# Last output tile of a hybrid trunk kernel: three column parts instead of two, and each last chunk scaled by two engines

## What is computed

```python
x = x + 0.5 * swiglu(rms_norm(x, g_ffn1), w_ffn1_gate, w_ffn1_up, w_ffn1_down)
y, st = hybrid_mixer(rms_norm(x, g_mix), ...)       # four mLSTM heads, four retention heads
x = x + y
x = x + 0.5 * swiglu(rms_norm(x, g_ffn2), w_ffn2_gate, w_ffn2_up, w_ffn2_down)
y_prompt, y_sample = rms_norm(x, g_final)           # x * rsqrt(mean(x*x) + eps) * g_final
```

## Time and profile before

| | us |
|---|---|
| median of 3 runs | 1085.72 |
| lowest and highest run | 1085.02, 1087.20 |
| the profiled execution, its own time | 1087.44 |
| its span in the profile | 1085.7 |
| PE busy | 1064.5 (98%) |
| DVE busy | 683.4 (63%) |
| ACT busy | 465.5 (43%) |
| POOL busy | 215.5 (20%) |

### The profile page before, as it was taken

One profiled execution on the slowest core, in us unless ns is written; L12 is line 12 of the kernel. 1 busy time (PEld: TensorE's weight loads), 2 busy tenths in 40 slices (PEclk: granted clock), 3 DMA queues, 4 the chain that ended last, 5 costly groups with the idle time before them and its releaser, 6 DMA issues.

```text
span 1085.7 us, 20465 instructions
## 1 busy us (share of the span) xinstructions
PE 1064.5 (98%) x8428; PEld 1059.2 (98%) x8428; DVE 683.4 (63%) x1142; ACT 465.5 (43%) x813; POOL 215.5 (20%) x182
## 2 busy tenths in 40 slices
PE   8989999999999999999999999999999999999997
PEld 7989999999999998999999999998999999999997
DVE  6798752367776675464655556578876235777544
ACT  7356641146663234333332223426665114666322
POOL 2332100022101220121222232224210002220111
PEclk9999999999999998999999999999999999999999
DMA  7479673288833375446444325537966428882422
GB/s 220 88 155 201 121 181 92 79 174 166 175 82 97 75 128 111 64 64 75 79 65 72 78 59 77 138 81 146 201 137 160 113 65 171 178 180 54 118 74 83
DMA packets 245061, 127.00 MB, mean 117 GB/s; under 512 B 9088, under 2 KB 243624, under 8 KB 244840
## 3 DMA queue, kind: packets, MB, share of 16 engines
q1 hardware_dynamic: 206952, 106.81, 41.0%
q0 software_dynamic: 38016, 18.88, 14.1%
HBM read 122.38 MB, written 3.28 MB: 116 GB/s over the span
## 4 chain that ended last, share of the span: by engine, by line
PE 87%; DVE 6%; issue 3%; ACT 2%; DMA 1%; SPq 0%; POOL 0%; ACTq 0%; DVEq 0%
PE dense L565 45%; PE dense L664 30%; PE core_banks L664 5%; ACT w_hi L944 1%; DVE x_hat L1372 1%; DVE rstd L1303 1%; PE core_banks L800 1%; PE core_banks L815 1%; DVE w_lo L1349 1%; PE core_banks L818 1%; PE core_banks L790 1%; PE core_banks L565 1%; PE dense L714 1%; DMA gain_rows<-in_g_gn_ret 1%; DVE h_f L1546 0%
## 5 line engine op out<-in xcount | busy, mean ns | idle before, releaser
L1292 DVE TENSOR_TENSOR w_lo<-w_raw,w_hi 128x1024 fp32r<-128x1024 f32 (+2 forms) x119 | 135.1, 1153 | 71.6 <-ACT w_hi L944 71.5
L565 PE MATMUL dense<-xg_hi,w_hi 128*128 128x272 f32 x768 | 163.2, 294 | 0.9 <-DVE xg_lo L1297 0.7
L565 PE MATMUL dense<-xg_lo,w_hi 128*128 128x272 f32 x768 | 159.3, 289 | 0.0
L565 PE MATMUL dense<-xg_hi,w_lo 128*128 128x272 f32 x768 | 159.1, 288 | 0.0
L944 ACT ACTIVATE w_hi<-w_raw 128x1024 fp32r<-128x1024 f32 (+2 forms) x120 | 107.2, 907 | 93.8 <-PE dense L565 82.4
L565 PE MATMUL dense<-h_hi,w_hi 128*128 128x272 f32 x684 | 142.4, 290 | 0.0
L565 PE MATMUL dense<-h_lo,w_hi 128*128 128x272 f32 x684 | 141.1, 287 | 0.0
L565 PE MATMUL dense<-h_hi,w_lo 128*128 128x272 f32 x684 | 140.9, 287 | 0.0
L664 PE MATMUL dense<-x_op_hi,w_hi 128*128 128x272 f32 x432 | 125.0, 289 | 5.1 <-ACT kept L1013 5.1
L664 PE MATMUL dense<-x_op_hi,w_lo 128*128 128x272 f32 x432 | 124.9, 289 | 0.0
L664 PE MATMUL dense<-x_late_hi,w_hi 128*128 128x272 f32 x432 | 124.5, 288 | 0.0
(11 more groups left out here) (299 smaller groups left out, 2138.9 us busy)
## 6 DMA issues: line engine op xcount, KB each, us to landing
w_src<-in_w_ffn_gate SPq DMA_DIRECT2D x90, 256.0 KB, 4.7
w_raw<-in_w_ffn_up SPq DMA_DIRECT2D x90, 256.0 KB, 3.5
w_raw<-in_w_in SPq DMA_DIRECT2D x32, 512.0 KB, 8.5
w_raw<-in_w_ffn_down SPq DMA_DIRECT2D x32, 384.0 KB, 4.1
w_raw<-in_w_ffn_down SPq DMA_DIRECT2D x32, 320.0 KB, 3.5
w_src<-in_w_ffn_gate POOLq DMA_DIRECT2D x36, 256.0 KB, 5.6
w_raw<-in_w_ffn_up POOLq DMA_DIRECT2D x36, 256.0 KB, 5.7
w_raw<-in_w_ffn_gate SPq DMA_DIRECT2D x8, 512.0 KB, 5.7
```

The lines of the kernel that those rows point to most:

```text
L565: last = nc.tensor.matmul(out[:, half, 0:TH], w[:, s % 4, k, :], x(kt)[:, half * TH:(half + 1) * TH], start=start and n == 0 and m == 0, s ...
L1292: nc.vector.tensor_tensor(w_lo[:, s % 4, 0:nk, :], w_raw[:, s % RAW, 0:nk, :], w_hi[:, s % 4, 0:nk, :].bitcast(F32), ALU.subtract).then_in ...
```

## The change

`LAST_CHUNKS` and `LAST_COLS` now cut the last tile in three parts: 288 tokens (chunks 2, 3, sample), 128 tokens (chunk 1) and 128 tokens (chunk 0). Part 2's products go to the other PSUM buffer (`last_out`), and chunk 1 is transposed into that buffer's second bank (`last_turned`). On PE the order becomes: part 0 with the transposes of tile 6 inside, part 1, `turn_last(0)`, the first unit of part 2, `turn_last(1)`, the second unit, `turn_last(2)`. In `turn_last` the product by `sq_sum` no longer waits for the newest squares, and part 2's waits for DVE's first copy and for the first root. On ACT the gain of part 1 comes ahead of the root of part 0. On DVE the residual add of part 1 comes ahead of part 0's copy and scaling. Chunks 1 and 0 are each scaled half by ACT (features 0 to 511) and half by DVE (512 to 1023), and SP stores in the order 2, 3, sample, 1, 0.

```diff
@@ -78,8 +78,8 @@
     X_PIECES = [(c, half) for c in X_ORDER for half in ((0, 1) if c < NC else (0,))]
 
 
-    LAST_CHUNKS = [(2, 3, NC), (0, 1)]
-    LAST_COLS = [slice(2 * P, T), slice(0, 2 * P)]
+    LAST_CHUNKS = [(2, 3, NC), (1,), (0,)]
+    LAST_COLS = [slice(2 * P, T), slice(P, 2 * P), slice(0, P)]
     RAW = 4
     T_F1 = 0
     T_GATE = T_F1 + TILES_F
@@ -311,6 +311,15 @@
                     quarter(1, 1))[o]
 
         X_NEEDS = (4, 9, 10, 8, 11, 12, 8)
+
+        def last_out(t, part):
+
+            tile = bank_of(t + part // 2)
+            return tile[:, part % 2, 0:LAST_COLS[part].stop - LAST_COLS[part].start]
+
+        def last_turned(part):
+
+            return bank_of(T_DOWN[1][1] + DT)[:, 1, :] if part == 1 else X[:, 2, :]
 
         def halves(tile):
             return tile[:, :, 0:TH]
@@ -540,8 +549,8 @@
 
             ffn(1, w_ffn2_gate, w_ffn2_up, w_ffn2_down)
 
-            for c in (2, 3, NC, 0, 1):
-                sp.wait_ge(y_done[c], 1)
+            for c in (2, 3, NC, 1, 0):
+                sp.wait_ge(y_done[c], 1 if c > 1 else 2)
                 if c < NC:
                     sp.dma_start(y_prompt[0, CH[c], :], y_tok[:, c, :]).then_inc(stored, 16)
                 else:
@@ -704,6 +713,8 @@
             def last_tile(s, t):
 
                 for part, cols in enumerate(LAST_COLS):
+                    if part == 2:
+                        tile_free(t + 1)
                     for u, (a, b) in enumerate(DOWN_K[1]):
                         if part == 0:
                             pe.wait_ge(w_lo_ready, s + u + 1)
@@ -711,27 +722,33 @@
                                 tile_free(t)
                         for kt in range(a, b):
                             for m, (w, x) in enumerate(((w_hi, h_hi), (w_hi, h_lo), (w_lo, h_hi))):
-                                last = nc.tensor.matmul(bank_of(t)[:, part, 0:cols.stop - cols.start], w[:, (s + u) % 4, kt - a, :],
+                                last = nc.tensor.matmul(last_out(t, part), w[:, (s + u) % 4, kt - a, :],
                                                         x[:, kt, cols], start=kt == 0 and m == 0, stop=kt == FC[1] - 1 and m == 2)
-                        if u == 0:
-                            turn_out(0, DT - 2) if part == 0 else turn_last(0)
+                        if u == 0 and part == 0:
+                            turn_out(0, DT - 2)
+                        if u == 0 and part == 2:
+                            turn_last(1)
                     last.then_inc(last_part_done, 1)
-                turn_last(1)
+                    if part == 1:
+                        turn_last(0)
+                turn_last(2)
 
             def turn_last(part):
 
                 pe.wait_ge(sq_added, DT * 3 - 1)
-                pe.wait_ge(sq_ready, DT * 3 + part)
-                pe.wait_ge(out_taken, DT - 1)
+                pe.wait_ge(out_taken, DT - 1 if part < 2 else DT)
+                if part == 2:
+                    pe.wait_ge(final_root, 1)
                 for c in LAST_CHUNKS[part]:
                     n = P if c < NC else TS
-                    nc.tensor.matmul(X[0:n, 0, c:c + 1], sq_sum[:, CH[c]], ones[:, 0:1], start=True, stop=False)
-                    last = nc.tensor.matmul(X[0:n, 0, c:c + 1], sq[:, CH[c]], ones[:, 0:1], start=False, stop=True)
+                    nc.tensor.matmul(X[0:n, part % 2, c:c + 1], sq_sum[:, CH[c]], ones[:, 0:1], start=True, stop=False)
+                    pe.wait_ge(sq_ready, DT * 3 + part)
+                    last = nc.tensor.matmul(X[0:n, part % 2, c:c + 1], sq[:, CH[c]], ones[:, 0:1], start=False, stop=True)
                 last.then_inc(final_sums, 1)
                 pe.wait_ge(x_gained, DT + part)
                 j = DT - 1
                 for c in LAST_CHUNKS[part]:
-                    out = X[:, 2, CH[c]] if c < NC else X[0:TS, 3, 0:P]
+                    out = last_turned(part)[:, CH[c]] if c < NC else X[0:TS, 3, 0:P]
                     last = nc.tensor.transpose(out, x_gain[:, j % 2, CH[c]], ident[:, :])
                 last.then_inc(out_turned, 1)
 
@@ -1106,8 +1123,15 @@
                     if c == 0:
                         continue
                     if n and j == DT - 1:
-                        for part in range(2):
-                            last_part(part)
+                        last_gain(0)
+                        last_gain(1)
+                        last_root(0)
+                        last_scale(0, 3, slice(0, D))
+                        last_root(1)
+                        last_scale(1, 1, slice(0, D // 2))
+                        last_gain(2)
+                        last_root(2)
+                        last_scale(2, 0, slice(0, D // 2))
                         return
                     if n == 0:
                         normed_hi(0, j, T_DOWN[n][c] + j, G_MIX, 0)
@@ -1120,24 +1144,31 @@
                         nc.scalar.activation(x_gain[:, j % 2, :], xT[:, j, :], ACT.Copy,
                                              scale=gains[:, G_FINAL + j:G_FINAL + j + 1]).then_inc(x_gained, 1)
 
-            def last_part(part):
-
-                cols, chunks = LAST_COLS[part], LAST_CHUNKS[part]
+            def last_gain(part):
+
+                cols = LAST_COLS[part]
                 act.wait_ge(last_part_taken, part + 1)
                 act.wait_ge(out_turned, DT - 2)
                 nc.scalar.activation(x_gain[:, (DT - 1) % 2, cols], xT[:, DT - 1, cols], ACT.Copy,
                                      scale=gains[:, G_FINAL + DT - 1:G_FINAL + DT]).then_inc(x_gained, 1)
+
+            def last_root(part):
+
+                chunks = [c for c in LAST_CHUNKS[part] if c < NC]
                 act.wait_ge(final_sums, part + 1)
-                a = chunks[0]
-                last = nc.scalar.activation(rms_tok[:, 0, a:a + 2], X[:, 0, a:a + 2], ACT.Sqrt, scale=1.0 / D, bias=eps[:, :])
-                if NC in chunks:
+                a, b = chunks[0], chunks[-1] + 1
+                last = nc.scalar.activation(rms_tok[:, 0, a:b], X[:, part % 2, a:b], ACT.Sqrt, scale=1.0 / D, bias=eps[:, :])
+                if part == 0:
                     last = nc.scalar.activation(rms_tok[0:TS, 0, NC:NC + 1], X[0:TS, 0, NC:NC + 1], ACT.Sqrt, scale=1.0 / D,
                                                 bias=eps[0:TS, :])
                 last.then_inc(final_root, 1)
+
+            def last_scale(part, c, cols):
+
                 act.wait_ge(final_rstd, part + 1)
-                act.wait_ge(out_taken, DT + part)
-                c = chunks[1]
-                nc.scalar.activation(y_tok[:, c, :], y_tok[:, c, :], ACT.Copy, scale=rms_tok[:, 1, c:c + 1])\
+                if cols.stop == D:
+                    act.wait_ge(out_taken, DT + part)
+                nc.scalar.activation(y_tok[:, c, cols], y_tok[:, c, cols], ACT.Copy, scale=rms_tok[:, 1, c:c + 1])\
                     .then_inc(y_done[c], 1)
 
 
@@ -1562,8 +1593,17 @@
                             block_to_lo(n, PAIRS[1][0], o + 1)
                     t = T_DOWN[n][c] + j
                     if n and c and j == DT - 1:
-                        for part in range(2):
-                            last_part(part, bank_of(t))
+                        last_residual(0, t)
+                        take_out(0, j - 1)
+                        last_residual(1, t)
+                        last_taken(0)
+                        last_scale(0, 2, slice(0, D))
+                        last_scale(0, NC, slice(0, D))
+                        last_taken(1)
+                        last_scale(1, 1, slice(D // 2, D))
+                        last_residual(2, t)
+                        last_taken(2)
+                        last_scale(2, 0, slice(D // 2, D))
                         return
                     add_residual(U_DOWN[n][c] + 2 * j + 1, 0, 0, j, bank_of(t), 0.5, 0)
                     if c == 0:
@@ -1583,35 +1623,39 @@
                 x = split_cols(xT[:, j + step * i, :])
                 nc.vector.scalar_tensor_tensor(x, halves(tile), factor, x, ALU.mult, ALU.add).then_inc(evicted, 1)
 
-            def last_part(part, tile):
-
-                cols, chunks, j = LAST_COLS[part], LAST_CHUNKS[part], DT - 1
+            def last_residual(part, t):
+
+                cols, j = LAST_COLS[part], DT - 1
                 dve.wait_ge(last_part_done, part + 1)
-                nc.vector.scalar_tensor_tensor(xT[:, j, cols], tile[:, part, 0:cols.stop - cols.start], 0.5, xT[:, j, cols],
+                nc.vector.scalar_tensor_tensor(xT[:, j, cols], last_out(t, part), 0.5, xT[:, j, cols],
                                                ALU.mult, ALU.add).then_inc(last_part_taken, 1)
                 dve.wait_ge(last_part_taken, part + 1)
                 dve.wait_ge(sq_added, DT * 3 - 1)
                 nc.vector.tensor_tensor(sq[:, cols], xT[:, j, cols], xT[:, j, cols], ALU.mult).then_inc(sq_ready, 1)
+
+            def last_taken(part):
+
```

(25 more changed lines are left out.)

## The result

| | before | changed |
|---|---|---|
| median, runs taken together | 1086.46 us (22 runs) | 1088.11 us (22 runs) |
| lowest and highest | 1084.88, 1088.49 | 1086.03, 1089.95 |
| span of the profiled execution | 1085.7 | 1087.4 |
| last tile's first product, from the span's start | 1067.24 | 1066.60 |
| from that product to the end of the span | 18.46 | 20.80 |

The ratio is 1.0015, 95% interval 1.0008 to 1.0022: the change makes the kernel about 1.6 us slower. That is under the 0.2% that the prediction took for measurable, and more than the 0.5 us it forecast. The median lies 0.1 us above the upper end of its range, 1088.0; the kernel before, too, ran 0.7 us slower in these 22 runs than in the 3 shown (1086.46 against 1085.72), so the difference of 1.65 against 0.5 is the fairer measure of the miss.

The account below looks back on a forecast made before the run. TensorE's products, the serial tail and the stores' bandwidth share the end. Products cost 3.0 us, the tail returns 2.5: 1086.2 us, 0.5 above the span of 1085.70; the range takes in 1084.6 and reaches 1088.0.

Parts of the forecast that it names:

- The spacing of narrow products: On TensorE in the last tile: sixty 128-column products 0.11 us apart, with bounds of 0.058 and 0.22.
- rival of 0.22: On TensorE, each of the sixty narrow products costs two records, 0.22 us apart; end at 1092.8; chance 0.11.
- rival of a hidden load: On TensorE, the weight load is hidden, so narrow products are 0.058 us apart; end at 1084.6; chance 0.12.
- 81 ns: The skill's figure for a 128-column product in a load-and-multiply stream; sixty would take 4.9 us, end at an estimated 1085.3.
- Second half 1.65, to 1080.51: On TensorE, part 2's second unit: fifteen 128-column products at 0.11 us take 1.65 us, ending at 1080.51.
- The tail: From the last residual add to the end: 5.47 us, of which 1.67 to the last scaling; before, 7.98.
- path A: TensorE's products, then the tail: last residual add at 1080.71, end at 1086.18, or 18.94 from the last tile's first product.
- Path B: The scaling: table load exposed, scaling starts at 1077.97, 1.6 us later; done 0.18 before the last residual add needs VectorE.
- rival of slipping scaling: Scaling slips by up to 1 us, VectorE takes the last residual late; end 1086.4 to 1087.2; chance 0.15.
- Path C: The stores: first issue at 1078.75, data from 1079.58, blocks of 3.06, 1.30 and 1.30, then 0.92; end at 1086.16.
- sign of being wrong: In the stores: a gap of over 0.5 us ahead of the last store would show the prediction wrong.
- split scaling: Last chunks scaled half by each engine: ScalarE's 512 columns take 0.72 us, VectorE's half, 0.38 to 0.75, hidden beside it.

Follow-up runs that it names:

- e1: The change with the sixty products of parts 1 and 2 over 256 columns instead of 128; ratio 1.0011, 19.63 us from the last tile's first product to the end.
- e4: The change with only part 2's thirty products over 256 columns, part 1's at 128; ratio 1.0011, 19.36 us from the last tile's first product to the end.
- e7: The kernel before with only the scaling by halves added, chunk 1 first; 18.38 us from the last tile's first product to the end, against 18.46.
- e11: The change without scaling by halves: ScalarE scales chunk 1 whole, VectorE chunk 0; 20.61 us from the last tile's first product to the end.
- e3: The change with only part 1's thirty products over 256 columns, part 2's at 128; ratio 1.0015, 20.80 us from the last tile's first product to the end.
- e10: e4 plus a one-element square root after ScalarE's first gain, loading its table there; 19.00 us from the last tile's first product to the end, instead of 19.36.
- e9: The change with chunk 1's sums and transpose moved behind part 2's two units, VectorE and ScalarE reordered; 19.13 us from the last tile's first product to the end.
- e13: The kernel of e9 again, timed against the kernel before; ratio 1.0007, 19.04 us from the last tile's first product to the end.
- e2: The kernel before with each 256-column product of its second part issued as two of 128; ratio 1.0024, 21.03 us from the last tile's first product to the end.

## Why the prediction was right in most steps and wrong in one, the clock

- **The spacing of narrow products**, the step with the widest bounds: 0.11 forecast, 0.111 measured. The rival of 0.22 was wrong for the reason given, and so was the rival of a hidden load; the 81 ns of the Trainium skill ("TensorE: Matmul & The Clock Gate", section "Back-to-back issue gap") were not seen: the 128-column float32r products are 0.111 us apart at the full clock in every kernel here that has them.
- **The clock**: this is the step that failed. "Second half 1.65, to 1080.51" priced fifteen products at the full clock, because the clock was full in the earlier trace rows and fell only in the tail in the earlier trace rows. They took 3.11, 1.46 more, and the last residual add came at 15.03 instead of 13.47. Nothing in the prediction asked what narrow products and sums between them do to the granted clock. The Trainium skill ("TensorE: Matmul & The Clock Gate", section "Part 1: The HAM clock gate") puts the half clock down to an idle engine. Here the clock fell while the records of TensorE stood back to back, so that rule, taken as written, would not have warned either, and the measurement decides.
- **The tail**: 5.47 forecast, 20.80 - 15.03 = 5.77 measured. The difference is the low clock again: from the last residual add to the last scaling the forecast had 1.67, the change has 17.04 - 15.03 = 2.01, and e1, at the full clock, has 1.66. The chain of e1 has 0.38 for the pair of sums and 0.18 for the transpose where the change has 0.59 and 0.33.
- Together 1.56 + 0.30 = 1.86 us, which is all of 20.80 - 18.94.
- **With the clock kept** the forecast of path A holds: e4's last residual add at 13.62, less 30 x 0.006 for its wider products, is 13.44 against 13.47. The kernel would still be slower than before, since e4's tile takes 19.36 against 18.46.
- **Path B**: scaling at 10.75 against 10.73, and both engines free before the last residual add, in e4 too, where VectorE waits 0.67 us for it; the rival of slipping scaling was wrong.
- **Path C**: first issue 11.53 against 11.51, but 5.66 us for the stores back to back was too little. In e4 they take from 12.4 to 18.4, 6.0 us, and hold its end: with the clock kept, this term would have been the one to miss. In the change itself it hides behind the late products, and the DMA engines stand idle for a microsecond ahead of the last store, which is over the 0.5 us that the prediction named as a sign of being wrong:

```profile
1084.15:1085.15 1.00, 0.00 (x0) 0.00 (x0) 0.00 (x0) 0.21 (x1) 0.00 (x0) 0.50 0.00 0
1085.15:1085.40 0.25, 0.00 (x0) 0.00 (x0) 0.00 (x0) 0.00 (x0) 0.00 (x0) 0.50 0.84 344
```

- **The split scaling** was priced right, 0.72 for ScalarE's half, but only against ScalarE's whole chunk of 1.15. Against VectorE's whole chunk of 0.75 it is worth nothing, and e7 and e11 show nothing.

Left open: why the clock falls at just that place. The runs show which work brings it and which does not; how much less than in the change would be enough was not tried, nor the sums without the transpose.

## What to carry to other kernels

When a change makes a busy engine's instructions smaller, price them twice, at the granted clock of now and at half of it, and look at the granted clock first in the profile after: a stretch that is busy in every record can still lose it. Cutting a tile finer pays at its consumers and costs at TensorE once the weight load sets the spacing, so cut the tail and leave the products whole. On a kernel of a thousand microseconds whose start wanders by two, measure a change at the end from a mark just ahead of it.

## What the runs showed of the hardware

- TensorE's clock fell to 1.2 GHz with no gap in its records, at 11.4 to 11.7 us in five profiles (the change three times, e3, e11), during one-column sums and a transpose behind 15 narrow products and an earlier set of sums; it stayed up when the 15 products were 256 wide (e1, e4, e10) or the second set of sums was elsewhere (e9, e13).
- At the low clock the narrow products are 3.11 / 15 = 0.207 us apart, 1.9 times 0.111: what sets their spacing, by the prediction's reading the weight load, slows with the clock.
- A 256-column float32r product costs 0.117 us and a 128-column one 0.111: half the columns save 5%.
- Two accumulations opened in turn, side by side in one PSUM bank (e2), left the prompt's output off by a relative 0.036; nothing else was changed against the kernel before. Which of the two pieces is wrong was not looked at.
